# Gate and up products of the last two token blocks as seven Strassen products, with block 1's feed-forward shared out over two mixes

## The chip, the cores and the metric

The kernel runs on one core of one Trainium2 chip. The metric is the device time of one execution in microseconds (us), lower is better. Of the kernel before there are three timed runs and one profiled execution.

## The reference, cut to what matters

The reference is one layer of a hybrid decoder. A prompt of 2048 tokens and a sample group of 64 tokens go through the same weights, all in float32. Per layer, on h of 1024 columns:

```python
z, xbc, dt_raw, q, k, v = split(rmsnorm(h, g_mix) @ w_in)
mix = concat(ssd_branch(z, xbc, dt_raw, ...), swa_banded(q, k, v, sinks, rel_bias))
h = h + mix @ w_out
h = h + cross_attention(rmsnorm(h, g_cross), mem_k, mem_v, w_cq, w_co)
hn = rmsnorm(h, g_ffn)
h = h + (silu(hn @ w_gate) * (hn @ w_up)) @ w_down      # 1024 -> 2816 -> 1024
y = rmsnorm(h, g_final)
```

The last-but-one line, the feed-forward, is what the change is about. Both kernels must give y of both groups and the new states and caches.

## The kernel before, in words

**Numbers as pairs.** A float32 operand is held as a high part (rounded to the fp32r format) and the rest, so each 128x128 piece of a product takes three TensorE matmuls of 512 columns: high x high, rest x high, high x rest (`multiply`, L2642 to L2644). Tokens are the 512 moving columns. Activations stand with the feature on the partition.

**Blocks.** The prompt is cut into four blocks of 512 tokens (0 to 3). A block has the stages I (input projection), mix (SSD scan and window attention), W (w_out), Q (cross query), cross attention, O (w_co), F (feed-forward: gate and up for each of 22 slices f of 128 hidden features, and `down` in groups of four slices, FG).

**Panels.** All weights come in panels of up to 1024 columns: SyncE loads a panel into `w_raw` (ring of three), ScalarE rounds it into `w_hi` (`round_panel`, L1641), VectorE takes the rest into `w_lo` (`low_panel`, L2037). Both do this two panels ahead of TensorE (AHEAD), at the head of each step of the order that `panel_order` writes out.

**Hosted work.** The mix of block b+1 is cut into 37 beats: `chain(ssd(b + 1), attention(b + 1))`, 19 beats for the scan and 18 for the attention. Each engine runs one beat after each step of block b's feed-forward, which has 66 steps (44 gate or up, 22 down), most of them 24 matmuls. So blocks 0, 1 and 2 host the mixes of blocks 1, 2 and 3.

**An attention unit** u (of 8) has an A beat and a B beat. In A, TensorE transposes the probabilities of unit u-1 (L2768) and forms the scores of unit u (L2783). VectorE adds the bias (L2276), takes maxima (L2284 to L2290), and ScalarE takes four exponentials (L1781). In B, VectorE normalises (L2299, semaphore `pn`, for which the transposes of the next A wait) and TensorE multiplies unit u-1 with the values (L2795). All queues run in program order:

```python
for p, step in enumerate(STEPS):           # ScalarE
    round_panel(n + AHEAD)
    if late is not None: round_hidden(late) # hid_h of the slice finished a step before
    ...                                     # silu of a gate step
    if p >= 1: next(mix, None)              # one beat
```

**Last block.** Block 3's feed-forward has nothing to host. `last_ffn` runs it alone, with panels of four outputs and two k, and works the sample group's 64 tokens through the same panels (`sample`, L2934 and L2935; `turn_sample`). Before it stands the third norm: squares and their sums (L1653, L2066), token sums (L2659), the reciprocal root and the diagonal (L2080), its row (L2664, L2085), then `norm3_t`, `norm3_hi`, `norm3_lo` (L2374, L1852, L2379).

**Engines besides.** GpSimd has almost nothing to do after the start: two copies and subtractions (L701, L705, L1627, L1629). Block b's y is turned and stored in the W stage of block b+1 (`turn_y`), block 3's at the end.

## Time and profile before

| what | us |
| --- | --- |
| timed runs: median (lowest to highest of 3) | 2883.46 (2878.35 to 2885.44) |
| span of the profiled execution | 2881.1 |
| what lies around it, if that execution took the median | 2.4 |
| TensorE matmul busy | 2775.2 (96%) |
| VectorE busy | 1561.8 (54%) |
| ScalarE busy | 1170.1 (41%) |
| GpSimd busy | 33.8 (1%) |
| HBM read and written | 277.90 MB and 23.85 MB, 105 GB/s |

The profile is one execution. The busy time of an engine is the union of its instructions. A matmul's time in a row runs from its start to its modelled end, so it is longer than the distance to the next one, which is what counts for throughput. PEclk is the granted clock of TensorE, 1.00 for 2.4 GHz and 0.50 for 1.2 GHz. A time in square brackets is what the engine was idle before the instruction, with the instruction that released it.

### The profile page before, as it was taken

The numbers are of one execution on the slowest core, as the hardware profiler recorded it, in microseconds if no ns is written. First come the engines' busy times: TensorE is split into PE (matmuls) and PEld (weight loads), VectorE is DVE, ScalarE is ACT, GpSimd is POOL, SyncE is SP. The second block draws the span as 40 slices with busy tenths as digits, with TensorE's granted clock in tenths as the row PEclk, the third lists the DMA queues.
The fourth block names the chain that finished last, engine by engine and source line by source line (L and its number), as shares of the span: only waits on it lengthen the run. The fifth ranks groups of instructions, "written<-read, shape, count | busy, mean of one in ns | idle before, by whom it ended". The sixth has DMA issues, their size and how long they took to land. (4 is left out here: it accounts for less than half of the span.)

```text
span 2881.1 us, 34707 instructions
## 1 busy us (share of the span) xinstructions
PE 2775.2 (96%) x13539; PEld 2248.0 (78%) x13539; DVE 1561.8 (54%) x2591; ACT 1170.1 (41%) x1878; POOL 33.8 (1%) x53
## 2 busy tenths in 40 slices
PE   6799789999999999999999999999999987999998
PEld 4478667888878888888778888888778876888886
DVE  4455665667653386667553576666643555333334
ACT  3455644543452255443542246444532333222222
POOL 2100000000000000000000000000000000000000
PEclk9899989999999999999999999999999998999998
DMA  9643554222223354222223353222223331222221
GB/s 306 228 127 117 168 144 124 81 82 76 81 72 92 100 176 110 81 84 74 74 88 95 103 172 99 82 73 80 75 88 99 119 122 52 80 81 81 81 81 60
DMA packets 415094, 303.05 MB, mean 105 GB/s; under 512 B 48075, under 2 KB 384079, under 8 KB 413890
## 3 DMA queue, kind: packets, MB, share of 16 engines
q1 hardware_dynamic: 412474, 294.41, 33.9%
q10 hardware_dynamic: 1880, 6.34, 0.6%
q8 instruction: 108, 1.77, 0.3%
q14 instruction: 56, 0.46, 0.1%
q0 software_dynamic: 576, 0.07, 0.0%
HBM read 277.90 MB, written 23.85 MB: 105 GB/s over the span
## 5 line engine op out<-in xcount | busy, mean ns | idle before, releaser
L2037 DVE TENSOR_TENSOR w_lo<-w_raw,w_hi 128x1024 fp32r<-128x1024 f32 x398 | 486.6, 1224 | 526.4 <-ACT w_hi L1641 524.7
L1641 ACT ACTIVATE w_hi<-w_raw 128x1024 fp32r<-128x1024 f32 x398 | 419.2, 1054 | 538.0 <-PE L L2644 260.5
L2642 PE MATMUL L<-xa_h,w_hi 128*128 128x512 f32 x1184 | 474.3, 401 | 0.0
L2643 PE MATMUL L<-xa_h,w_lo 128*128 128x512 f32 x1184 | 463.6, 392 | 0.0
L2644 PE MATMUL L<-xa_l,w_hi 128*128 128x512 f32 x1184 | 463.3, 391 | 0.0
L2642 PEld LDWEIGHTS L<-xa_h,w_hi 128*128 128x128 f32 x1184 | 223.6, 189 | 54.0 <-issue 6.7
L2644 PEld LDWEIGHTS L<-xa_l,w_hi 128*128 128x128 f32 x1184 | 223.5, 189 | 48.0
L2643 PEld LDWEIGHTS L<-xa_h,w_lo 128*128 128x128 f32 x1184 | 223.7, 189 | 45.9 <-issue 1.0
L2642 PE MATMUL L<-xb_h,w_hi 128*128 128x512 f32 x576 | 230.8, 401 | 9.6 <-DVE xb_l L2056 9.6
L2644 PE MATMUL L<-xb_l,w_hi 128*128 128x512 f32 x576 | 225.6, 392 | 0.0
L2643 PE MATMUL L<-xb_h,w_lo 128*128 128x512 f32 x576 | 225.5, 392 | 0.0
L2642 PE MATMUL L<-hid_h,w_hi 128*128 128x512 f32 x528 | 210.9, 399 | 1.2 <-DVE hT L2596 1.2
L2643 PE MATMUL L<-hid_h,w_lo 128*128 128x512 f32 x528 | 206.1, 390 | 0.0
L2644 PE MATMUL L<-hid_l,w_hi 128*128 128x512 f32 x528 | 205.9, 390 | 0.0
L2596 DVE TENSOR_TENSOR hT<-L,hT 128x512 f32<-128x512 f32 x144 | 99.4, 690 | 137.0 <-PE L L2644 136.5
L2954 PE MATMUL G<-xa_h,w_hi 128*128 128x512 f32 x352 | 139.0, 395 | 3.1 <-DVE xa_l L2379 3.1
L2955 PE MATMUL G<-xa_h,w_lo 128*128 128x512 f32 x352 | 138.4, 393 | 0.0
L2956 PE MATMUL G<-xa_l,w_hi 128*128 128x512 f32 x352 | 138.2, 392 | 0.0
L2642 PEld LDWEIGHTS L<-xb_h,w_hi 128*128 128x128 f32 x576 | 108.8, 189 | 35.0 <-POOL flip L1624 6.7
L2644 PEld LDWEIGHTS L<-xb_l,w_hi 128*128 128x128 f32 x576 | 108.8, 189 | 23.3
L2643 PEld LDWEIGHTS L<-xb_h,w_lo 128*128 128x128 f32 x576 | 109.0, 189 | 21.3 <-issue 0.7
L2642 PEld LDWEIGHTS L<-hid_h,w_hi 128*128 128x128 f32 x528 | 99.1, 188 | 28.1 <-issue 3.5
(570 smaller groups left out, 4518.5 us busy)
## 6 DMA issues: line engine op xcount, KB each, us to landing
w_raw<-in_w_down_dram SPq DMA_DIRECT2D x88, 512.0 KB, 3.4
w_raw<-in_w_gate_dram SPq DMA_DIRECT2D x66, 512.0 KB, 3.8
w_raw<-in_w_up_dram SPq DMA_DIRECT2D x66, 512.0 KB, 3.8
w_raw<-in_w_in_dram SPq DMA_DIRECT2D x56, 512.0 KB, 3.8
xt<-xT_dram SPq DMA_DIRECT2D x56, 256.0 KB, 3.9
w_raw<-in_w_gate_dram SPq DMA_DIRECT2D x44, 256.0 KB, 2.8
w_raw<-in_w_up_dram SPq DMA_DIRECT2D x44, 256.0 KB, 3.1
fwin<-in_w_in_dram SPq DMA_DIRECT2D x8, 1156.0 KB, 10.2
```

The costliest lines, as they stand in the source:

```text
L1641: act.activation(w_hi[:, n % RING, 0:w], w_raw[:, n % RING, 0:w], ACT.Copy)\
L2037: dve.tensor_tensor(w_lo[:, n % RING, 0:w], w_raw[:, n % RING, 0:w], w_hi[:, n % RING, 0:w].bitcast(F32), ALU.subtract).then_inc(s["lo_rea ...
L2596: dve.tensor_tensor(hT[:, n, :], bank(bank_of[o]), hT[:, n, :], ALU.add)\
L2642: pe.matmul(acc, wh, rh, start=(k == 0), stop=False)
L2643: pe.matmul(acc, wl, rh, start=False, stop=False)
L2644: last = pe.matmul(acc, wh, rl, start=False, stop=(k == kn - 1))
L2954: pe.matmul(bank(m), wh, rh, start=(first and k == 0), stop=False)
L2955: pe.matmul(bank(m), wl, rh, start=False, stop=False)
L2956: last = pe.matmul(bank(m), wh, rl, start=False, stop=(final and k == 2 * qs - 1))
```

## The change

**Order of blocks.** Block 0's feed-forward hosts block 1's mix as before. Block 1's feed-forward is cut in two: slices 0 to 10 host the mix of block 2, slices 11 to 21 that of block 3 (FORDER[1] and FORDER[2], 34 steps each, groups of 4, 4 and 3 slices, so that four of the down steps have 18 matmuls). The 37 beats fit in 33 steps because four steps (TWO_BEATS) take two beats. Block 1's normed input and h go to DRAM and come back (`xah_dram`, `xal_dram`, `h_dram`); block 2's normed input goes to DRAM as `xn_dram`.

**Gate and up of blocks 2 and 3 together.** After block 3's O stage, 22 units (a unit is 256 columns of w_gate or of w_up) are each taken as a 2x2 block product: the weights' quadrants are a half of the input features by 128 outputs, the activations' quadrants a half of the features by one of the two token blocks. Seven products of quadrant sums (p1 to p7, 12 matmuls each) replace eight. Of the weights, GpSimd forms four sums per unit (`sums`). Of the activations, four sums per k (`mixed`) are formed once, from block 2's normed input out of DRAM and block 3's from `third`. The results are put together by VectorE (`put_c11`, `put_c12`, `put_c21`, `put_c22`), the hidden values go to DRAM (`store_hidden`).

**Down of blocks 2 and 3** follows, each with its own pass over w_down (stage D), one block's 22 slices accumulated in PSUM. The hidden values come back from DRAM and are split again. The sample group's gate and up are worked out once per unit with 256 columns in place of 512 (`sample_unit`). Block 2's y is turned within block 3's down.

What each part is: `load_unit` loads 1 MB of raw weights, ScalarE's `unit_hi` and VectorE's `unit_lo` split them (`ghi`, `glo`), `sum_hi` and `sum_lo` split the four sums.

```diff
+FG = {0: [(0, 4), (4, 8), (8, 12), (12, 16), (16, 20), (20, 22)],
+      1: [(0, 4), (4, 8), (8, 11), (11, 15), (15, 19), (19, 22)]}
+FORDER = {0: ([("gu", f) for f in range(0, 5)] + [("d", 0)] + [("gu", f) for f in range(5, 9)] + [("d", 1)]
+              + [("gu", f) for f in range(9, 13)] + [("d", 2)] + [("gu", f) for f in range(13, 17)] + [("d", 3)]
+              + [("gu", f) for f in range(17, 22)] + [("d", 4), ("d", 5)]),
+          1: ([("gu", f) for f in range(0, 5)] + [("d", 0)] + [("gu", f) for f in range(5, 9)] + [("d", 1)]
+              + [("gu", 9), ("gu", 10), ("d", 2)]),
+          2: ([("gu", f) for f in range(11, 16)] + [("d", 3)] + [("gu", f) for f in range(16, 20)] + [("d", 4)]
+              + [("gu", 20), ("gu", 21), ("d", 5)])}
+FFN_OF = {0: 0, 1: 1, 2: 1}
...
-            order += [("E", b, step) for step in last_steps()]
+            order += [("F", FFN_OF[b], step) for step in ffn_steps(b)]
+    for b in (2, 3):
+        order += [("D", b, (half, q)) for half in range(2) for q in range(DQ)]
     return order
 
...
+            TWO_BEATS = (21, 24, 27, 30)
+            def mix_beats(b, p):
+                return 0 if p == 0 else 2 if b >= 1 and p in TWO_BEATS else 1
...
+                def load_unit(u):
+                    if u >= 2:
+                        sp.wait_ge(s["u_S"], FROM["u_S"] + 4 * (u - 1))
+                        sp.wait_ge(s["u_lo"], FROM["u_lo"] + 2 * (u - 1))
+                    w = w_up if u % 2 else w_gate
+                    c0 = (u // 2) * 256
+                    sp.dma_start(uraw[u % 2][:], w[:, c0:c0 + 256].rearrange("(k p) n -> p k n", p=P))\
+                      .then_inc(s[f"u_in{u % 2}"], 16)
...
+                    if A0 + 14 <= n < A0 + 14 + KT:
+                        k = n - A0 - 14
+                        sp.wait_ge(s["n3_l"], 2 * KT)
+                        sp.dma_start(xah_dram.ap()[:, k * TB:k * TB + TB], xa_h[:, k, :].bitcast(F32))\
+                          .then_inc(s["xa_out"], 16)
+                        sp.dma_start(xal_dram.ap()[:, k * TB:k * TB + TB], xa_l[:, k, :].bitcast(F32))\
+                          .then_inc(s["xa_out"], 16)
...
+                    if 0 <= n - pos[("I", 3, ("v", 0))] < 4:
+                        m = n - pos[("I", 3, ("v", 0))]
+                        if m == 0:
+                            sp.wait_ge(s["xa_out"], 32 * KT)
+                            sp.wait_ge(s["o_lo"], 3 * C)
+                        for part, there in ((xa_h, xah_dram), (xa_l, xal_dram)):
+                            sp.dma_start(part[:, 2 * m:2 * m + 2, :].bitcast(F32),
+                                         there.ap()[:, 2 * m * TB:2 * (m + 1) * TB].rearrange("p (k t) -> p k t", t=TB))\
+                              .then_inc(s["xa_in"], 16)
...
+                def sums(u):
+                    raw = uraw[u % 2]
+                    a11, a12, a21, a22 = raw[:, 0:4, 0:P], raw[:, 4:8, 0:P], raw[:, 0:4, P:256], raw[:, 4:8, P:256]
+                    s1, s2, s3, s4 = (Sr[:, i, :].rearrange("p (k n) -> p k n", n=P) for i in range(4))
+                    pool.wait_ge(s[f"u_in{u % 2}"], FROM[f"u_in{u % 2}"] + 16 * (u // 2 + 1))
+                    if u >= 1:
+                        pool.wait_ge(s["c_lo"], FROM["c_lo"] + 4 * u)
+                    pool.tensor_tensor(s1, a21, a22, ALU.add).then_inc(s["u_S"], 1)
+                    pool.tensor_tensor(s3, a11, a21, ALU.subtract).then_inc(s["u_S"], 1)
+                    pool.wait_ge(s["u_S"], FROM["u_S"] + 4 * u + 1)
+                    pool.tensor_tensor(s2, s1, a11, ALU.subtract).then_inc(s["u_S"], 1)
+                    pool.wait_ge(s["u_S"], FROM["u_S"] + 4 * u + 3)
+                    pool.tensor_tensor(s4, a12, s2, ALU.subtract).then_inc(s["u_S"], 1)
+                def mixed(i):
+                    o = stg[i % 2]
+                    b11, b21 = x2p[:, 2 * (i % 2), :], x2p[:, 2 * (i % 2) + 1, :]
+                    for e in range(2):
+                        pool.wait_ge(s[f"x2_in{2 * (i % 2) + e}"], 16 * (i // 2 + 3))
+                    if i >= 2:
+                        pool.wait_ge(s["t_lo"], FROM["t_lo"] + 5 * (i - 1))
+                    pool.wait_ge(s["x3_t"], FROM["x3_t"] + 2 * i + 1)
+                    pool.tensor_tensor(o["T1"][:], o["B12"][:], b11, ALU.subtract).then_inc(s["bt"], 1)
+                    pool.wait_ge(s["x3_t"], FROM["x3_t"] + 2 * i + 2)
+                    pool.tensor_tensor(o["T3"][:], o["B22"][:], o["B12"][:], ALU.subtract).then_inc(s["bt"], 1)
+                    pool.wait_ge(s["bt"], FROM["bt"] + 4 * i + 1)
+                    pool.tensor_tensor(o["T2"][:], o["B22"][:], o["T1"][:], ALU.subtract).then_inc(s["bt"], 1)
+                    pool.wait_ge(s["bt"], FROM["bt"] + 4 * i + 3)
+                    pool.tensor_tensor(o["T4"][:], b21, o["T2"][:], ALU.subtract).then_inc(s["bt"], 1)
...
+                    if b == 2:
+                        act.dma_start(xn_dram.ap()[:, i, :], T2[:, i % 2, :]).then_inc(s[f"xn_out{i % 2}"], 16)
+                        return
...
+                def mixed_hi(i):
+                    for n, name in enumerate(("B22", "T1", "T3", "T2", "T4")):
+                        if n == 0:
+                            act.wait_ge(s["x3_t"], FROM["x3_t"] + 2 * i + 2)
+                        else:
+                            act.wait_ge(s["bt"], FROM["bt"] + 4 * i + n)
+                        act.activation(xc_h[name][:, i, :], stg[i % 2][name][:], ACT.Copy).then_inc(s["t_hi"], 1)
...
+                def third(i):
+                    o = stg[i % 2]
+                    if i >= 2:
+                        dve.wait_ge(s["bt"], FROM["bt"] + 4 * (i - 1))
+                        dve.wait_ge(s["t_lo"], FROM["t_lo"] + 5 * (i - 1))
+                    for e, name in enumerate(("B12", "B22")):
+                        k = i + 4 * e
+                        dve.scalar_tensor_tensor(o[name][:], hT[:, k, :], g_of(PV_FFN, k), RB, ALU.mult, ALU.mult)\
+                           .then_inc(s["x3_t"], 1)
+                def mixed_lo(i):
+                    for n, name in enumerate(("B22", "T1", "T3", "T2", "T4")):
+                        dve.wait_ge(s["t_hi"], FROM["t_hi"] + 5 * i + n + 1)
+                        dve.tensor_tensor(xc_l[name][:, i, :], stg[i % 2][name][:], xc_h[name][:, i, :].bitcast(F32),
+                                          ALU.subtract).then_inc(s["t_lo"], 1)
...
+                def put_c22(u):
+                    j = u // 2
+                    dve.wait_ge(s["p5"], FROM["p5"] + u + 1)
+                    dve.wait_ge(s["u3_ev"], FROM["u3_ev"] + u + 1)
+                    dve.wait_ge(s["c21_ev"], FROM["c21_ev"] + u + 1)
+                    if u % 2 == 0:
+                        dve.wait_ge(s["h_out2"], FROM["h_out2"] + 16 * j)
+                        dve.tensor_tensor(gq[:, 2, :], u3[:], bank(5), ALU.add).then_inc(s["c22_ev"], 1)
+                    else:
+                        dve.tensor_tensor(u3[:], u3[:], bank(5), ALU.add).then_inc(s["c22_ev"], 1)
+                        dve.wait_ge(s["g_ev"], FROM["g_ev"] + 4 * j + 3)
+                        dve.drain()
+                        dve.tensor_tensor(gq[:, 2, :], gq[:, 2, :], u3[:], ALU.mult).then_inc(s["h_ev"], 1)
...
+                def product(acc, w, x, ks, begin, end, more_on=False):
+                    for k in ks:
+                        wh, wl = w(k)
+                        xh, xl = xc_h[x][:, k, :], xc_l[x][:, k, :]
+                        pe.matmul(acc, wh, xh, start=(begin and k == 0), stop=False, skip_group_check=more_on)
+                        pe.matmul(acc, wl, xh, start=False, stop=False, skip_group_check=more_on)
+                        last = pe.matmul(acc, wh, xl, start=False, stop=(end and k == 3), skip_group_check=more_on)
+                    return last
...
+                def p1(u):
+                    pe.wait_ge(s["u_lo"], FROM["u_lo"] + 2 * u + 1)
+                    if u % 2 == 0 and u >= 2:
+                        pe.wait_ge(s["g_ev"], FROM["g_ev"] + 4 * (u // 2 - 1) + 1)
+                    elif u >= 3:
+                        pe.wait_ge(s["h_ev"], FROM["h_ev"] + 4 * ((u - 3) // 2) + 1)
+                    product(bank(u % 2), own(0, 0), "B11", ALL, True, True).then_inc(s["p1"], 1)
+                def p2(u):
+                    pe.wait_ge(s["u_lo"], FROM["u_lo"] + 2 * u + 2)
+                    pe.wait_ge(s["t1_ev"], FROM["t1_ev"] + u + 1)
+                    product(bank(u % 2), own(1, 0), "B21", ALL, False, True, True).then_inc(s["p2"], 1)
+                def p3(u):
+                    pe.wait_ge(s["c_lo"], FROM["c_lo"] + 4 * u + 4)
+                    pe.wait_ge(s["c22_ev"], FROM["c22_ev"] + u + 1)
+                    product(bank(5), mixed(3), "B22", ALL, False, True, True).then_inc(s["p3"], 1)
...
+                def p6(u, ks=ALL):
+                    pe.wait_ge(s["c_lo"], FROM["c_lo"] + 4 * u + 1)
+                    if u >= 1:
+                        pe.wait_ge(s["u2_ev"], FROM["u2_ev"] + u)
+                    return product(bank(3), mixed(0), "T2", ks, True, True)
...
+                def gate_up():
+                    for i in range(4):
+                        pe.wait_ge(s["t_lo"], FROM["t_lo"] + 5 * (i + 1))
+                        for fn, sem in ((p4, "p4"), (p6, "p6"), (p7, "p7"), (p5, "p5")):
+                            last = fn(0, range(i, i + 1))
+                            if i == 3:
+                                last.then_inc(s[sem], 1)
+                    for u in range(1, UNITS):
+                        p1(u)
+                        p3(u - 1)
+                        p4(u).then_inc(s["p4"], 1)
+                        p2(u)
+                        sample_unit(u)
+                        p6(u).then_inc(s["p6"], 1)
+                        p7(u).then_inc(s["p7"], 1)
+                        if u % 2 == 1:
+                            turn_sample(u // 2)
+                        p5(u).then_inc(s["p5"], 1)
+                    p3(UNITS - 1)
```

The instruction order shows what moved. `L2596` and `L3101`, `L2037` and `L2392`, `L2299` and `L2658`, `L2276` and `L2635` are the same lines before and after.

VectorE in the feed-forward of block 1, from the bias addition of attention unit 2 to that of unit 3 (first the kernel before):

```order
L2276 TENSOR_TENSOR SC<-G,bias 128x1024
L2284 TENSOR_REDUCE sm<-SC 128x4
L2287 TENSOR_TENSOR sm<-sm,snk 128x4
L2289 TENSOR_SCALAR sm<-sm 128x4
L2290 TENSOR_TENSOR sm<-snk,sm 128x4
L2596 TENSOR_TENSOR hT<-L,hT 128x512 x2
L2037 TENSOR_TENSOR w_lo<-w_raw,w_hi 128x1024
L2295 TENSOR_TENSOR sm<-sm 128x4
L2297 RECIPROCAL sm<-sm 128x4
L2299 TENSOR_TENSOR SC<-SC,sm 128x1024
L2306 TENSOR_TENSOR q_l<-G,q_h 128x2x128
L2037 TENSOR_TENSOR w_lo<-w_raw,w_hi 128x1024
```

```order
L2643 TENSOR_REDUCE sm<-SC 128x4
L2646 TENSOR_TENSOR sm<-sm,snk 128x4
L2648 TENSOR_SCALAR sm<-sm 128x4
L2649 TENSOR_TENSOR sm<-snk,sm 128x4
L3101 TENSOR_TENSOR hT<-L,hT 128x512 x2
L2392 TENSOR_TENSOR w_lo<-w_raw,w_hi 128x1024
L2654 TENSOR_TENSOR sm<-sm 128x4
L2656 RECIPROCAL sm<-sm 128x4
L2658 TENSOR_TENSOR SC<-SC,sm 128x1024
L2665 TENSOR_TENSOR q_l<-G,q_h 128x2x128
L2635 TENSOR_TENSOR SC<-G,bias 128x1024
```

Before, a whole step (its `w_lo` is the last row) stood between unit 2's normalisation and unit 3; now unit 3 follows at once.

ScalarE at the end of slice 10, the last before group d2 (`down` of slices 8 to 10), in the changed kernel. `SC,sm` are the exponentials of attention unit 6, the second `hid_h` is slice 10:

```order
L2027 ACTIVATE PT<-G 128x1024
L2031 ACT_TABLE_LOAD
L2031 ACTIVATE SC,sm<-SC,sm 128x256 x4
L2033 ACTIVATE sm<-sm 128x4
L1891 ACTIVATE w_hi<-w_raw 128x768
L2351 ACTIVATE hid_h<-sg 128x512
L2039 ACTIVATE q_h<-G 128x2x128
```

Before, the down groups inside block 1's feed-forward used slices that were at least a step older:

```order
L1777 ACTIVATE PT<-G 128x1024
L1781 ACTIVATE SC,sm<-SC,sm 128x256 x4
L1783 ACTIVATE sm<-sm 128x4
L1641 ACTIVATE w_hi<-w_raw 128x1024
L1789 ACTIVATE q_h<-G 128x2x128
```

The rounding of slice 10 now stands behind the exponentials and a panel, and the down step that reads it stands next on TensorE.

VectorE after block 3's third norm. Before, the pairs of `norm3_t` and `norm3_lo`, and now `third` and `mixed_lo` (`st_` and `x2p` are raw sums and block 2's input, `xh_`, `xl_` their parts):

```order
L2379 TENSOR_TENSOR xa_l<-T_96,xa_h 128x512
L2374 SCALAR_TENSOR_TENSOR T_96<-hT,pv,diag 128x512
L2379 TENSOR_TENSOR xa_l<-T_96,xa_h 128x512
L2374 SCALAR_TENSOR_TENSOR T_96<-hT,pv,diag 128x512
L2379 TENSOR_TENSOR xa_l<-T_96,xa_h 128x512 x2
```

```order
L2790 SCALAR_TENSOR_TENSOR st_B_168<-hT,pv,diag 128x512
L2790 SCALAR_TENSOR_TENSOR st_B_169<-hT,pv,diag 128x512
L2796 TENSOR_TENSOR xl_B_135<-st_B_163,xh_B_128 128x512
L2796 TENSOR_TENSOR xl_T_136<-st_T_164,xh_T_129 128x512
L2796 TENSOR_TENSOR xl_T_138<-st_T_165,xh_T_131 128x512
L2796 TENSOR_TENSOR xl_T_137<-st_T_166,xh_T_130 128x512
L2796 TENSOR_TENSOR xl_T_139<-st_T_167,xh_T_132 128x512
```

For each of four k there are now two products and five remainders on VectorE, with the four sums on GpSimd between them.

## Rows read from the trace of the kernel before

**Rows 1.** The page: busy time, share of the span and instructions.
```profile
PE 2775.2 (96%) x13539; PEld 2248.0 (78%) x13539; DVE 1561.8 (54%) x2591; ACT 1170.1 (41%) x1878; POOL 33.8 (1%) x53
```
**Rows 2.** Windows: us, busy of PE, PEld, DVE, ACT, POOL, PEclk, DMA share, GB/s.
```profile
2000.00:2100.00 100.00, 100.00 (x530) 78.24 (x529) 61.14 (x96) 56.89 (x112) 0.00 (x0) 1.00 0.24 72
...
2428.40:2850.00 421.60, 421.60 (x1899) 341.28 (x1898) 145.04 (x183) 107.75 (x146) 0.00 (x0) 1.00 0.24 77
```
**Rows 3.** Timeline of PE, start and us, 24 matmuls of 512 columns apart (W stage).
```profile
2303.56 0.39 PE L2642 MATMUL L<-ym_h,w_hi 128*128 128x512 f32 x1
...
2309.00 0.39 PE L2642 MATMUL L<-ym_h,w_hi 128*128 128x512 f32 x1
```
**Rows 4.** Timeline of DVE: attention units 0, 1 and 4 of block 3's mix.
```profile
2006.29 1.23 DVE L2276 TENSOR_TENSOR SC<-G,bias 128x1024 f32<-128x1024 f32 x1 [2.74 <-PE G L2783]
...
2014.73 1.23 DVE L2299 TENSOR_TENSOR SC<-SC,sm 128x1024 f32<-128x1024 f32 x1
...
2019.23 1.23 DVE L2276 TENSOR_TENSOR SC<-G,bias 128x1024 f32<-128x1024 f32 x1
...
2027.15 1.23 DVE L2299 TENSOR_TENSOR SC<-SC,sm 128x1024 f32<-128x1024 f32 x1
...
2061.79 1.23 DVE L2276 TENSOR_TENSOR SC<-G,bias 128x1024 f32<-128x1024 f32 x1 [2.10 <-PE G L2783]
...
2070.22 1.23 DVE L2299 TENSOR_TENSOR SC<-SC,sm 128x1024 f32<-128x1024 f32 x1
```
**Rows 5.** Timeline of PE in block 2's feed-forward: the same units 0 and 1.
```profile
2006.17 0.50 PE L2642 MATMUL L<-xa_h,w_hi 128*128 128x512 f32 x1
...
2011.79 0.39 PE L2642 MATMUL L<-hid_h,w_hi 128*128 128x512 f32 x1
...
2017.26 1.03 PE L2768 MATMUL G<-ident,SC 128*128 128x128 f32 x8
...
2024.83 1.08 PE L2795 MATMUL G<-PT,vtok 128*64 128x256 f32 x8
```
**Rows 6.** Timeline of ACT, unit 4: rounding of a panel and of a hidden slice.
```profile
2066.93 1.04 ACT L1641 ACTIVATE w_hi<-w_raw 128x1024 fp32r<-128x1024 f32 x1
...
2069.86 0.63 ACT L1997 ACTIVATE hid_h<-sg 128x512 fp32r<-128x512 f32 x1
```
**Rows 7.** Windows around the idle times of PE in block 3, columns as in rows 2.
```profile
2325.00:2329.00 4.00, 0.48 (x4) 0.06 (x2) 2.64 (x4) 2.19 (x3) 0.00 (x0) 1.00 0.41 131
2329.50:2336.30 6.80, 6.80 (x19) 5.54 (x20) 2.84 (x16) 0.00 (x0) 0.00 (x0) 0.50 0.00 0
...
2414.80:2428.40 13.60, 7.05 (x14) 4.24 (x15) 10.12 (x25) 3.29 (x6) 0.00 (x0) 0.50 0.00 1
```
**Rows 8.** Timeline of PE from block 3's last O matmul to its feed-forward.
```profile
2410.46 0.39 PE L2644 MATMUL L<-cq_l,w_hi 128*128 128x512 f32 x1
...
2423.42 0.76 PE L2954 MATMUL G<-xa_h,w_hi 128*128 128x512 f32 x1 [3.10 <-DVE xa_l L2379]
```
**Rows 9.** Timeline of DVE at the end of the third norm, blocks 3 and 2.
```profile
2420.36 0.69 DVE L2085 COPY diag<-G 128x512 f32<-128x512 f32 x1 [2.17 <-PE G L2664]
...
1862.27 1.23 DVE L2037 TENSOR_TENSOR w_lo<-w_raw,w_hi 128x1024 fp32r<-128x1024 f32 x1 [0.26 <-ACT w_hi L1641]
```
**Rows 10.** DMA issues: KB each, median us to landing.
```profile
xt<-xT_dram SPq DMA_DIRECT2D x56, 256.0 KB, 3.9
...
mem<-in_mem_prompt_dram SPq DMA_DIRECT2D x1, 1024.0 KB, 5.5
```
**Rows 11.** Groups of POOL, mean ns and idle before; then DVE's timeline beside L1629.
```profile
L701 POOL TENSOR_TENSOR stT<-stT,edS 128x512 f32<-128x512 f32 x8 | 8.0, 1039 | 22.9 <-DVE xS L999 22.9
...
L1629 POOL TENSOR_TENSOR kml<-kmT,kmh 128x1024 fp32r<-128x1024 f32 x1 | 3.2, 3233 | 0.1
...
232.20 1.73 DVE L2037 TENSOR_TENSOR w_lo<-w_raw,w_hi 128x1024 fp32r<-128x1024 f32 x1
```

1047 lines of the change are left out of this document (720 added, 327 removed).

## The prediction

> **What bounds the kernel now.** I read the page's busy times first. TensorE is busy 96% of the span; VectorE 54%, ScalarE 41%, GpSimd 1% [rows 1]. So the kernel runs at TensorE's pace, unless a stage says otherwise. The windows say the same by stage: while block 2's feed-forward hosts attention TensorE is busy 100 of 100 us at clock 1.00, with VectorE at 61 and ScalarE at 57; in block 3's lone feed-forward it is busy 421.6 of 421.6 us with VectorE at 145 [rows 2]. There a matmul less is time less. Twenty-four matmuls of 512 columns lie (2309.00 - 2303.56) / 24 = **0.2267 us** apart [rows 3]; that is the price of one. What TensorE loses, it loses between the stages, by gaps and by the clock after them; and the hosted stages stay full only because the chain of the attention is covered. These two the change touches.
>
> **The change part by part.**
>
> *Products.* Gate and up of blocks 2 and 3 were 2 x 44 steps of 24 = 2112 matmuls; now 22 units x 7 x 12 = 1848. 264 x 0.2267 = **-59.9 us**. The sample's 176 matmuls fewer of 512 columns are replaced by 352 of half the width: nothing. Nothing else on TensorE is dropped: block 1's gate, up and down, and down of blocks 2 and 3, are the same matmuls in another order. Does TensorE stay the bound within the units? A unit is 84 x 0.2267 + 16 x 0.113 = 20.9 us. VectorE has two remainders of 1024 columns, four of 512 and six or seven sums of 512 out of PSUM, at 1.23 and 0.69 about 10.5 us; GpSimd four sums of 512, 4.2 us at 1.04 (that price is argued below); ScalarE less than VectorE. Yes, by a factor of two.
>
> *Attention with less cover: +42.* Before, two steps lie between one unit's scores and the next unit's transposes; at TWO_BEATS only one does. The chain from the bias addition to the end of the normalisation is 2006.29 to 2014.73 + 1.23 = 9.67 us for unit 0, 9.15 for unit 1, 9.66 for unit 4, in which hidden slices are rounded too [rows 4]. TensorE's cover is one step, 2006.17 to 2011.79 = 5.6, and the product with the values, 1.08 (none beside unit 0) [rows 5]. So TensorE waits 9.67 - 5.6 = 4.1 at p = 21, 9.15 - 6.7 = 2.45 at p = 24 and 9.66 - 6.7 = 3.0 at p = 27. Queued behind the waiting transposes is the next unit's score and with it its chain, so the loss isn't caught up. At p = 30 two things meet. Group d2 stands right behind slice 10, whose `hid_h` waits on ScalarE for unit 6's exponentials and a panel: in the row of unit 4 ScalarE is free of both 2066.93 + 1.04 - 2061.79 = 6.2 us after the addition [rows 6]; with `hid_h` 0.63 and the remainder 0.69 it is 7.5. TensorE comes to slice 10 after six matmuls, 1.5 us: 6.0 lost. VectorE's additions of that delayed step then stand ahead of unit 6's normalisation: an estimated 2.5 more. The last remainder of the attention, for which W waits, adds 1.7. Together 4.1 + 2.45 + 3.0 + 6.0 + 2.5 + 1.7 = 20 per host; the second host's d5 also has the squares for the norm, 1.0 each: 22. Bounds: 30, if the chain loses a third where TensorE waits; 50, if VectorE's panel remainder is always caught behind the additions.
>
> *The clock after a gap: +13.6.* In the W stage of block 3 TensorE did 0.48 of 4.00 us at clock 1.00; the stretch behind it, 6.8 us, ran at 0.50, that is 1.2 GHz [rows 7]. It costs half of itself, 3.4. I count the two gaps of each host that are over 3.5 us (4.1 and 6.0), 4 x 3.4. Bounds 0 (hosted gaps lie too far apart to matter) and 24 (seven gaps do).
>
> *From the third norm to gate and up: +16.4.* Before: 2423.42 - 2410.46 = 12.96 us idle [rows 8] and 13.6 us at 0.50 about it, of which I put 2.5 to work done at the low clock: 15.4 [rows 7]. Now VectorE has the norm's row at 2420.36 + 0.69, 10.6 after the last O matmul [rows 9]. Behind it stand three `sum_lo` (3 x 0.69) and the first `third` (0.75), with 0.6 for the hand-overs: T1 starts at 14.0. Then 16 GpSimd operations in a row, 16 P. Unit 1 can't be loaded before, since block 2's input lies where its weights go: 1 MB, 5.5 us to landing [rows 10], rounding 1.04, remainder 1.23. TensorE has 72 matmuls of unit 0 and its sample part to do meanwhile, 18.1 us. Lost: 14.0 + 16 P + 7.8 - 18.1 + 2.5 = 6.2 + 16 P. P is 1.04 in GpSimd's one group of 512 columns; beside a remainder on VectorE, 1024 columns took 3.23, half of that is 1.6, and VectorE's own remainder stretched from 1.23 to 1.73 [rows 11]. Here VectorE is working all the time, so P = 1.6: 31.8 - 15.4 = **+16.4**. By P = 1.04 it would be +7.4. The upper bound is mutual exclusion: in each k, VectorE's 5 x 0.69 + 2 x 0.75 = 4.95 on top of 4 x 1.04 makes 2.27 per sum: +27. The Trainium skill speaks against the change here, in "GPSIMD Engine Reference", section "8. Key points": GpSimd and VectorE share their interface to SBUF and contend when VectorE reads two SBUF inputs. By that rule mutual exclusion, the upper bound, would hold, and GpSimd would be a poor home for sums on the critical path; rows 11 agree that both stretch, though by less than full exclusion.
>
> *The rest: +3.* Block 1's normed input goes out and comes back in 256 KB pieces (3.9 us to landing [rows 10]) while hundreds of steps lie between: 0. Block 2's third norm must wait for its stores before a buffer of `T2` is used again; its last panel remainder ends at 1863.5 [rows 9], 4.5 before TensorE's next need: 0 to 5, I take 1.5. The turn from gate and up to down: the last `put_c22` and the store and return of the hidden values; down begins with slices that are long there: 1.5 at the end for filling PSUM banks. DMA traffic rises by some tens of MB, on queues at 0.24 of their time [rows 2]: nothing.
>
> Sum: -59.9 + 42 + 13.6 + 16.4 + 3 = **+15.1**. Against the profiled execution 2881.1 + 15.1 = 2896.2 of span; that execution stands 2.4 under the median of the runs, which I add: **2898.5 us**. A measurement of this kernel tells about 0.3% (8.7 us) from no change: faster is below 2875, slower above 2892.
>
> **The rivals.**
>
> *A, the attention hides itself: 2854.* The place is the one step at p = 21, 24, 27 and 30. The chain of 9.66 holds a panel's rounding and remainder and a hidden slice (1.04 + 1.23 + 0.63 = 2.9). If these do not stand on it, it is 6.8, just the 6.7 that TensorE has to do; that is the point from which it decides. Then per host 1.2 + 0.1 + 0.1 + 3.1 + 2.5 + 1.7, some 9 to 10, so 20 in all, and no gap is long enough for the clock. With the prologue at P = 1.04: -59.9 + 20 + 7.4 + 3 = -29.5. For it: matmuls saved are certain, and all else is slack. Against it: in the order of both engines panel and hidden slice do stand between exponentials and normalisation.
>
> *B, a wash: 2876 to 2890.* Waits as forecast, but the clock stays up (0) and P = 1.04: -59.9 + 42 + 7.4 + 3 = -7.5 (2876); with one of the two as forecast, up to 2889.6. For it: the gaps of the hosts are 20 us apart with full work between; the fall in [rows 7] is at a change of stage.
>
> *C, GpSimd and VectorE exclude each other: 2928.* P = 2.27 in the prologue (+27), the units' sums stretch but stay hidden, and each of seven gaps per host drops the clock (24) with waits at the upper bound (50): -59.9 + 50 + 24 + 27 + 3 = +44.
>
> That the change doesn't do what it says is out: the order has 264 matmuls of these fewer and the two-beat steps as described.
>
> **How the numbers follow.** Forecast 0.46 (2885 to 2912 on its own), A 0.22, B 0.22, C 0.10. Of the forecast's 0.46 I give 0.40 to slower and 0.06, its lower end, to no change; of B's 0.22 0.20 to no change and 0.02 to faster; A is faster, C slower. Faster 0.22 + 0.02 = 0.24, same 0.06 + 0.20 = 0.26, slower 0.40 + 0.10 = 0.50. The range goes from 2858, which leaves out half of A, to 2928, which leaves out half of C.
>
> **What would show it.** TensorE's instructions: gate and up of blocks 2 and 3 at 20.9 us per unit, full. In each host four gaps before L3274 of about 4, 2.5, 3 and 2.5 us, ended by VectorE's L2658, and one of 6 inside d2 and d5 ended by the `hid_l` of slices 10 and 21, two of the five with the clock at 0.50 behind them. From block 3's O to the first products: T1 14 us after the last O matmul, 16 sums on GpSimd at 1.6 each. The forecast is wrong if L3274 doesn't wait after a two-beat step, if the sums take 1.04 beside VectorE, or if TensorE waits within the units (then GpSimd or VectorE is the bound there, which none of the cases holds).

## The result, and the profile after

| what | before | after |
| --- | --- | --- |
| median of the runs (lowest to highest) | 2882.06 us (2878.35 to 2885.44, 4 runs) | 2911.56 us (2910.02 to 2913.88, 4 runs) |
| span of the profiled execution | 2881.1 us | 2912.2 us |
| TensorE matmul busy | 2775.2 us | 2736.2 us |
| ratio after / before, 95% interval | | 1.0108 [1.0093, 1.0123] |

The changed kernel is 29.5 us slower. The forecast was 2898.5, within a range of 2858 to 2928, so the sign was right and the size half; the result lies at the very top of what the forecast had as its own case (2885 to 2912). The page, with the lines that answer to [rows 1]:

```profile
PE 2736.2 (94%) x13451; PEld 2224.2 (76%) x13451; DVE 1609.2 (55%) x2679; ACT 1179.0 (40%) x1948; POOL 172.6 (6%) x157
...
PE   6799789999999999999889999889769999989998
...
PEclk9899999999999999999999999999889999999999
```

TensorE is busy for 39 us less, and the span is 31 us longer. (Its work fell by more, 61 us by the table below; matmuls at the low clock last longer.) The row of PE shows where to look: the two pairs of 8 are the ends of the two hosted halves of block 1's feed-forward, the 7 and 6 are block 3's cross attention and the start of gate and up, the 8 that follows them is the turn to down. The windows of these stretches, columns as in [rows 2]:

```profile
1380.00:1500.00 120.00, 100.66 (x502) 76.76 (x501) 63.99 (x104) 48.85 (x111) 0.00 (x0) 0.90 0.20 59
1850.00:1972.00 122.00, 100.16 (x509) 76.42 (x509) 71.33 (x120) 53.91 (x120) 0.00 (x0) 0.93 0.15 46
2170.00:2600.00 430.00, 430.00 (x2088) 362.83 (x2087) 196.56 (x280) 130.58 (x210) 100.81 (x80) 1.00 0.22 74
```

The units themselves are full: 430 of 430 us at clock 1.00, VectorE at 46%, GpSimd at 23% with 100.81 / 80 = 1.26 us per sum. The hosted ends, full before, now lack some 20 us each and run at 0.90 and 0.93.

**Where the time went.** A matmul's usual distance to the next is that of most of its kind (0.227 us at 512 columns). What a stretch takes beyond the sum of these is lost. I split it into distances over 0.95 us (gaps), the excess of those under the clock of 0.50, and the small rest:

| stretch | forecast | measured | how it comes out of the two traces |
| --- | --- | --- | --- |
| matmuls | -59.9 | -60.8 | sum of the usual distances, 2643.0 before, 2582.2 after |
| gaps in the two hosts | +42 | +42.3 | 20.0 (1380 to 1500) + 22.3 (1850 to 1972), none before |
| low clock in the two hosts | +13.6 | +22.8 | 13.2 + 9.6, none before |
| third norm to gate and up | +16.4 | +22.7 | 34.2 (2104.6 to 2170) less 11.5 (2410.5 to 2430 before); the first wait behind O, 2.3 in both, is left out of both |
| turn to down | +3, with all the rest | +10.3 | 2600 to 2630 |
| rest | | -6.2 | mostly small distances in the attention, 12.9 + 12.9 before, 8.9 + 10.4 after |
| sum | +15.1 | +31.1 | 2912.2 - 2881.1 |

The lines between these terms are not sharp. With the usual distance taken by line, tiles and shape of the matmul, as their median, the same traces give -62.1 for the matmuls, and for the two hosts 44.3 of gaps and 19.5 of low clock: 63.8 in all, beside the 65.1 of the table.

**The gaps in the host.** Timeline of TensorE, the matmul after each of the five largest gaps in the first host, with what ended the wait:

```profile
1386.72 0.69 PE L3274 MATMUL G<-ident,SC 128*128 128x128 f32 x2 [4.05 <-DVE SC L2658]
...
1415.20 0.55 PE L3274 MATMUL G<-ident,SC 128*128 128x128 f32 x3 [2.52 <-DVE SC L2658]
...
1442.60 0.55 PE L3274 MATMUL G<-ident,SC 128*128 128x128 f32 x3 [3.07 <-DVE SC L2658]
...
1467.56 0.80 PE L3148 MATMUL L<-hid_h,w_hi 128*128 128x512 f32 x1 [5.71 <-DVE hid_l L3074]
...
1476.32 0.55 PE L3274 MATMUL G<-ident,SC 128*128 128x128 f32 x3 [1.90 <-DVE SC L2658]
```

The waits were forecast at 4.1, 2.45, 3.0, 6.0 and 2.5. The fourth ends with the remainder of slice 10, the others with VectorE's normalisation, as named. The sixth, forecast at 1.7 before W, is a distance of 1.66 at 1496.7. ScalarE and VectorE at that fourth wait:

```profile
1464.84 0.49 ACT L2031 ACTIVATE SC<-SC,sm 128x256 f32<-128x256 f32 x1
1465.24 0.19 ACT L2031 ACTIVATION_READ_ACCUMULATOR SC<-SC,sm 128x1 f32 x1
1465.34 0.19 ACT L2033 ACTIVATE sm<-sm 128x4 f32<-128x4 f32 x1
1465.43 0.83 ACT L1891 ACTIVATE w_hi<-w_raw 128x768 fp32r<-128x768 f32 x1
1466.16 0.61 ACT L2351 ACTIVATE hid_h<-sg 128x512 fp32r<-128x512 f32 x1
```

```profile
1460.30 1.23 DVE L2635 TENSOR_TENSOR SC<-G,bias 128x1024 f32<-128x1024 f32 x1 [1.03 <-PE G L3289]
...
1466.81 0.69 DVE L3074 TENSOR_TENSOR hid_l<-sg,hid_h 128x512 fp32r<-128x512 f32 x1 [3.49 <-ACT hid_h L2351]
```

The hidden slice is rounded behind the exponentials and a panel, and its remainder ends 1466.81 + 0.69 - 1460.30 = 7.2 us after the bias addition; 7.5 was forecast.

**From the third norm to the units.** GpSimd's first sum, the two it had to wait for and the last, then VectorE: the products of the first two k and the remainders of the first:

```profile
2117.62 1.64 POOL L1867 TENSOR_TENSOR st_T<-st_B,x2p 128x512 f32<-128x512 f32 x1 [14.10 <-DVE st_B L2790]
...
2131.67 1.64 POOL L1867 TENSOR_TENSOR st_T<-st_B,x2p 128x512 f32<-128x512 f32 x1 [0.72 <-DVE st_B L2790]
...
2140.51 1.63 POOL L1867 TENSOR_TENSOR st_T<-st_B,x2p 128x512 f32<-128x512 f32 x1 [2.17 <-DVE st_B L2790]
...
2145.59 1.59 POOL L1873 TENSOR_TENSOR st_T<-x2p,st_T 128x512 f32<-128x512 f32 x1
```

```profile
2116.70 4.78 DVE L2790 SCALAR_TENSOR_TENSOR st_B<-hT,pv,diag 128x512 f32<-128x512 f32 x4
2121.40 1.75 DVE L2796 TENSOR_TENSOR xl_B<-st_B,xh_B 128x512 fp32r<-128x512 f32 x1
2123.07 6.75 DVE L2796 TENSOR_TENSOR xl_T<-st_T,xh_T 128x512 fp32r<-128x512 f32 x4
```

The first sum starts 2117.62 - 2104.51 = 13.1 us after the last O matmul (14.0 forecast); a sum takes 1.67 (1.6 forecast). But VectorE pays more: in the first k its remainders take 6.75 / 4 = 1.69 us in place of some 0.6, and GpSimd then waits for it twice (0.72 and 2.17). In the second and third k, where GpSimd stands still for a part of the time, four of them take 5.70 and 5.72 us, and in the last, with GpSimd silent, 2.48. So the sixteen sums last 29.6 us, 1.85 each.

A second part of this stretch came out longer than forecast. From the end of the last sum (2145.59 + 1.59 = 2147.18) to the first matmul of unit 1 (2159.15) it is 12.0 us, where the forecast has 7.8. SyncE, ScalarE, VectorE and TensorE on this way:

```profile
2147.21 0.38 SPq L1615 DMA_DIRECT2D uraw<-in_w_up_dram  x1
...
2152.03 1.28 ACT L2154 ACT_TABLE_LOAD   x1
...
2154.30 2.01 ACT L2129 ACTIVATE ghi<-uraw 128x1024 fp32r<-128x1024 f32 x2 [0.38 <-issue]
...
2156.56 0.69 DVE L2848 TENSOR_TENSOR gq<-u,G 128x512 f32<-128x512 f32 x1
2157.17 3.06 DVE L2775 TENSOR_TENSOR glo<-uraw,ghi 128x1024 fp32r<-128x1024 f32 x2
...
2159.15 0.50 PE L3402 MATMUL G<-xh_B,ghi 128*128 128x512 f32 x1 [2.89 <-DVE glo L2775]
```

The weights are there for GpSimd at 2152.88, 5.7 after the issue, as forecast. But ScalarE comes to their rounding only at 2154.30, behind the function table and the gate of unit 0, and VectorE to the remainder at 2157.17, behind three results of unit 0.

**The turn to down.** TensorE's product p3 of the last unit needs `put_c22` (L2808). In VectorE's queue it stands behind the remainders of hidden slices 4 to 7, whose data SyncE had only just asked for:

```profile
2610.80 2.20 SPq L1628 DMA_DIRECT2D hraw<-hid_dram  x4
...
2613.51 0.63 ACT L2177 ACTIVATE xh_T<-hraw 128x512 fp32r<-128x512 f32 x1 [6.65 <-DMA hraw<-hid_dram]
2614.70 0.68 DVE L2870 TENSOR_TENSOR xl_T<-hraw,xh_T 128x512 fp32r<-128x512 f32 x1
...
2618.16 0.68 DVE L2808 TENSOR_TENSOR u<-u,G 128x512 f32<-128x512 f32 x1
...
2618.99 0.76 PE L3402 MATMUL G<-xh_B,sh_h 128*128 128x512 f32 x1 [7.58 <-DVE u L2808]
```

### The profile page after: what moved, and what is told of

It reads as the page before. It is cut to its first block and busy times, and to the rows that moved or that the text cites. A ratio compares the mean times of both kernels' runs of the same rounds, so it can differ in the third digit from the quotient of the medians.

```text
span 2912.2 us, 35273 instructions
## 1 busy us (share of the span) xinstructions
PE 2736.2 (94%) x13451; PEld 2224.2 (76%) x13451; DVE 1609.2 (55%) x2679; ACT 1179.0 (40%) x1948; POOL 172.6 (6%) x157
## 5 line engine op out<-in xcount | busy, mean ns | idle before, releaser
L2392 DVE TENSOR_TENSOR w_lo<-w_raw,w_hi 128x1024 fp32r<-128x1024 f32 (+1 forms) x312 | 379.4, 1217 | 373.8 <-ACT w_hi L1891 372.1
L1891 ACT ACTIVATE w_hi<-w_raw 128x1024 fp32r<-128x1024 f32 (+1 forms) x312 | 326.7, 1048 | 313.5 <-PE L L3150 124.3
L3148 PE MATMUL L<-xa_h,w_hi 128*128 128x512 f32 x832 | 334.8, 402 | 0.0
L3150 PE MATMUL L<-xa_l,w_hi 128*128 128x512 f32 x832 | 325.2, 391 | 0.0
L3149 PE MATMUL L<-xa_h,w_lo 128*128 128x512 f32 x832 | 325.0, 391 | 0.0
L3148 PEld LDWEIGHTS L<-xa_h,w_hi 128*128 128x128 f32 x832 | 156.6, 188 | 37.2 <-issue 4.7
L3150 PEld LDWEIGHTS L<-xa_l,w_hi 128*128 128x128 f32 x832 | 156.6, 188 | 34.0
L3149 PEld LDWEIGHTS L<-xa_h,w_lo 128*128 128x128 f32 x832 | 156.9, 189 | 32.0 <-issue 1.0
L3148 PEld LDWEIGHTS L<-xb_h,w_hi 128*128 128x128 f32 x576 | 109.2, 190 | 34.2 <-POOL flip L1838 6.7
L3101 DVE TENSOR_TENSOR hT<-L,hT 128x512 f32<-128x512 f32 x96 | 65.9, 689 | 85.3 <-PE L L3150 85.1
L3402 PE MATMUL G<-xh_T,sh_h 128*128 128x512 f32 x264 | 105.9, 401 | 0.0
L3404 PE MATMUL G<-xl_T,sh_h 128*128 128x512 f32 x264 | 104.8, 397 | 0.0
```

The lines of the kernel that those rows point to most:

```text
L1891: act.activation(w_hi[:, n % RING, 0:w], w_raw[:, n % RING, 0:w], ACT.Copy)\
L2392: dve.tensor_tensor(w_lo[:, n % RING, 0:w], w_raw[:, n % RING, 0:w], w_hi[:, n % RING, 0:w].bitcast(F32), ALU.subtract).then_inc(s["lo_rea ...
L3101: dve.tensor_tensor(hT[:, n, :], bank(bank_of[o]), hT[:, n, :], ALU.add)\
L3148: pe.matmul(acc, wh, rh, start=(k == 0), stop=False)
L3149: pe.matmul(acc, wl, rh, start=False, stop=False)
L3150: last = pe.matmul(acc, wh, rl, start=False, stop=(k == kn - 1))
```

## The experiments

All are the changed kernel with one edit or a sum of edits. Each is timed against runs of the kernel before on the same chip.

**1. The two-beat steps moved to the scan.**

```diff
-            TWO_BEATS = (21, 24, 27, 30)
+            TWO_BEATS = (6, 8, 10, 12)
...
-                        if p == GATED_ROOT:
+                        root = GATED_ROOT if b == 0 else GATED_ROOT - 4
+                        if p == root:
```

> The four steps with two beats are moved from the attention to the scan (p = 6, 8, 10, 12; the second and third beat of each chunk together). Theory (the attention's chain of 9.7 us has one step of cover instead of two): the gaps before L3274 of 2.9 to 4.5 us go, and with them most of the low clock of the two hosts; what stays is about 2 us at d2 and d5 and 2 before W, per host, and at most 1 to 2 us per scan chunk where the scan's own chain now has one step. Hosts lose some 15 us in gaps and clock in place of 65, so about 2862 us. Rival (the gaps come from more work per step on VectorE and ScalarE in the two hosts, wherever it stands): the gaps only move into the scan, and the time stays within 10 us of 2911.

Measured: 2877.64 us, 0.999 [0.998, 0.9999] of before, 34 us less than the changed kernel. No gap before L3274 is left; 2.3 us remain at d2 and d5 (6.1 before) and 1.7 and 2.3 before W. The rival falls: in the same stretches (1380 to 1500, 1840 to 1952) gaps cost 3.4 + 4.0 us and the low clock 1.5 + 1.5, so both go together. It missed 2862 by 15; a new gap of 5.1 us in each host, with the low clock behind it, makes up for these (2 x 4.9 us over the usual distance and 5.0 of low clock). VectorE there (idle times of TensorE at 1336.86 to 1341.97):

```profile
1333.93 0.69 DVE L2600 TENSOR_TENSOR zs<-yac,G 128x512 f32<-128x512 f32 x1
1335.79 0.17 DVE L2606 TENSOR_SCALAR ssg<-ssg 128x8 f32<-128x8 f32 x1 [1.17 <-ACT sqsum L2007]
...
1339.04 2.19 DVE L2612 TENSOR_SCALAR zs<-zs,ssg 128x256 f32<-128x256 f32 x8
1341.14 1.28 DVE L3102 TENSOR_TENSOR hT<-L,hT 128x512 f32<-128x512 f32 x2
```

The root of the gate is drawn ahead of the step's own work, and the step is now a down step, whose additions (L3102) free TensorE's banks.

**2. The same with the root at a gate step.**

```diff
-            TWO_BEATS = (6, 8, 10, 12)
+            TWO_BEATS = (6, 8, 10, 15)
...
-                        root = GATED_ROOT if b == 0 else GATED_ROOT - 4
+                        root = GATED_ROOT if b == 0 else GATED_ROOT - 3
```

> As e1, but the pairs are at p = 6, 8, 10 and 15 (the two turns of the scan's result together) and VectorE's root of the gate is drawn ahead at step 14, a gate step, in place of step 13, a down step. In e1 a gap of 5.1 us stood before step 14 in both hosts: VectorE worked on the root and eight scalings (5.4 us) ahead of the additions of step 13, for whose banks TensorE waited. Theory: that gap and its low clock go, 2 x (5.1 + 3) less 2, so 2877.6 - 13 = about 2864. Rival (the scan's pairs at p = 10 and 12 made it): a gap of like size at the same place or before the turns, about 2877.

Measured: 2866.94 us, 0.9956 [0.994, 0.9971]. The gap is gone and nothing took its place. So the hosting of two mixes by one feed-forward costs little when the pairs stand where the chains are short: in the hosted stretches 8.9 us of gaps and clock are left of 65, and by the medians the choice of the four steps was worth 2911.56 - 2866.94 = 44.6 us. That is less than the 56 us of gaps and clock that went; some 5 of these came back as small distances in the same stretches. The one wait left inside the first host, TensorE's timeline:

```profile
1452.46 0.50 PE L3149 MATMUL L<-hid_h,w_hi 128*128 128x512 f32 x1 [1.93 <-DVE hid_l L3074]
```

**3. The hidden slice ahead of the exponentials**, the pairs as in the changed kernel.

```diff
                         elif kind == "up":
                             late = f
+                            if b >= 1 and p == 29:
+                                round_hidden(late)
+                                late = None
```

> In the changed kernel, ScalarE rounds the hidden slice 10 (and 21) ahead of unit 6's exponentials and the next panel. Theory (the 6.1 us gaps inside d2 and d5 are that slice waiting on ScalarE behind the exponentials): they fall to 2 to 4 us, with some of the wait moving to unit 6's normalisation, 3 to 7 us less in all. Rival (VectorE's product and remainder, behind the bias addition and maxima, set it): the gaps stay at 5 to 6 us.

Measured, a single run: 2900.59 us beside 2911.56. The wait at d2, forecast at 2 to 4:

```profile
1464.19 0.50 PE L3151 MATMUL L<-hid_h,w_hi 128*128 128x512 f32 x1 [2.14 <-DVE hid_l L3077]
```

The distances fell from 6.1 to 2.5 in both hosts, 7.2 us, and unit 6's wait stayed (2.6 and 3.0). The theory holds, but the 11 us are more than the 3 to 7 it gave. The traces have the low clock for the rest: each gap of 6.1 us in the changed kernel has 6.8 us at 0.50 with it, and neither gap of 2.5 us here has any. How much of the 11 us a second run would repeat isn't known.

**4. The activation sums on VectorE.** GpSimd's `mixed` goes; in `third`:

```diff
+                    b11, b21 = x2p[:, 2 * (i % 2), :], x2p[:, 2 * (i % 2) + 1, :]
+                    for e in range(2):
+                        dve.wait_ge(s[f"x2_in{2 * (i % 2) + e}"], 16 * (i // 2 + 3))
+                    dve.drain()
+                    dve.tensor_tensor(o["T1"][:], o["B12"][:], b11, ALU.subtract).then_inc(s["bt"], 1)
+                    dve.tensor_tensor(o["T3"][:], o["B22"][:], o["B12"][:], ALU.subtract).then_inc(s["bt"], 1)
+                    dve.drain()
+                    dve.tensor_tensor(o["T2"][:], o["B22"][:], o["T1"][:], ALU.subtract).then_inc(s["bt"], 1)
+                    dve.drain()
+                    dve.tensor_tensor(o["T4"][:], b21, o["T2"][:], ALU.subtract).then_inc(s["bt"], 1)
```

> The sixteen activation sums are formed by VectorE instead of GpSimd. Theory (the two engines slow each other: 1.69 us per operation on both sides): VectorE's remainders fall back to 0.69 and its sums take 0.69; per k it has 11 operations, 7.7 us, in place of the 8.7 of now; unit 1 is loaded some 6 us sooner, 5 to 9 us less, about 2904. Rival (VectorE's remainders are slow from something else, such as where their operands lie): they stay at 1.69, VectorE's stretch grows to 4 x 13 us, and the time rises by 10 to 15 us.

Measured: 2906.31 us, 1.0089 [1.0074, 1.0104], 5 us less than the changed kernel. VectorE in the second k:

```profile
2121.82 0.69 DVE L2778 TENSOR_TENSOR st_T<-st_B,x2p 128x512 f32<-128x512 f32 x1
...
2124.59 0.68 DVE L2788 TENSOR_TENSOR xl_B<-st_B,xh_B 128x512 fp32r<-128x512 f32 x1
2125.20 2.49 DVE L2788 TENSOR_TENSOR xl_T<-st_T,xh_T 128x512 fp32r<-128x512 f32 x4
```

With GpSimd silent the same four remainders take 2.49 us, not 6.75. One engine with eleven operations is faster here than two that share them: counted from the last O matmul, the last sum ends 6.9 us sooner and unit 1 begins 6.4 us sooner. The rival falls.

**5. The two engines in turn**, neither beside the other: GpSimd's sums wait for both products of their k, VectorE's remainders for all four sums, and the products of the next k stand behind the remainders.

```diff
-                    pool.wait_ge(s["x3_t"], FROM["x3_t"] + 2 * i + 1)
+                    pool.wait_ge(s["x3_t"], FROM["x3_t"] + 2 * i + 2)
...
                 def mixed_lo(i):
+                    dve.wait_ge(s["bt"], FROM["bt"] + 4 * (i + 1))
...
-                    for i in range(5):
-                        if i < 4:
-                            third(i)
-                        if i >= 1:
-                            mixed_lo(i - 1)
+                    for i in range(4):
+                        third(i)
+                        mixed_lo(i)
```

> In the changed kernel GpSimd's four sums of a k and VectorE's seven operations of it are put one behind the other, never side by side (VectorE's remainders wait for all four sums, and the next k begins when they are done). Theory (the two engines take their turns at one interface: beside each other 4 of each took 6.75 us, alone 4 x 0.62 + 4 x 1.04 = 6.6): each sum falls from 1.67 to about 1.04 us, each remainder from 1.69 to 0.62, and nothing is lost by not overlapping: the 16 sums end within 3 us of the 29.6 us they take now, and the time stays within 5 us of the changed kernel. Rival (they only slow each other in part, overlap still gains): a sum alone takes 1.3 or more, and the stretch grows by over 5 us.

Measured, a single run: 2918.39 us, 6.8 more than the changed kernel; beside the one run of the kernel before on its chip (2885.36) it is 33.0 more, where the changed kernel had 29.5. GpSimd, then VectorE, in the second k:

```profile
2128.54 1.27 POOL L1867 TENSOR_TENSOR st_T<-st_B,x2p 128x512 f32<-128x512 f32 x1 [4.63 <-DVE st_B L2790]
2129.77 1.28 POOL L1869 TENSOR_TENSOR st_T<-st_B,st_B 128x512 f32<-128x512 f32 x1
```

```profile
2134.28 2.49 DVE L2797 TENSOR_TENSOR xl_T<-st_T,xh_T 128x512 fp32r<-128x512 f32 x4
```

A sum alone takes 1.27, not 1.04, and a remainder alone 0.62. So full exclusion would be 4 x (1.27 + 0.62) = 7.6 us for four of each; side by side they took 6.75. The sixteen sums now last 34.2 us (2118.85 to 2153.08), 4.7 more. Overlap of sums and remainders gains about a tenth, no more. The expectation (within 3 us, a sum at 1.04) fell, though the rival's 1.3 and 5 us were not reached either. Whether the whole kernel stays within 5 us a single run can't tell.

**6. The last `put_c22` ahead of the hidden slices.**

```diff
-                    for h in range(4):
-                        hidden_lo(h)
-                    low_panel(DFIRST, NPAN)
-                    low_panel(DFIRST + 1, NPAN)
-                    for h in range(4, 8):
-                        hidden_lo(h)
-                    put_c22(UNITS - 1)
+                    hidden_lo(0)
+                    hidden_lo(1)
+                    put_c22(UNITS - 1)
+                    low_panel(DFIRST, NPAN)
+                    hidden_lo(2)
+                    hidden_lo(3)
+                    low_panel(DFIRST + 1, NPAN)
+                    for h in range(4, 8):
+                        hidden_lo(h)
```

> Only VectorE's order at the turn from gate and up to down is changed: the last put_c22 and the first panel remainder stand before the remainders of hidden slices 2 to 7. Theory (the 7.97 us gap is VectorE standing in hidden_lo of slices 4 to 7, whose transfer had just been issued, ahead of the put_c22 that p3 of the last unit waits for): gap 1 to 3 us, no or a shorter low-clock stretch behind it, 6 to 9 us less, about 2904. Rival (TensorE waits for data of down, not for that queue order): p3 comes earlier but the same time is lost before the first matmul of down, 2911.

Measured: 2909.73 us, 1.0103 [1.0087, 1.0118]; 1.8 us less than the changed kernel, within what such medians scatter. The trace shows both halves of it: the gap of 7.97 is 1.26, and gaps of 2.07, 2.57 and 0.92 us stand in the first down steps. The queue order was the cause of the big gap, and most of the gain was given back.

**7. Both last puts ahead.** On top of 6:

```diff
                     low_panel(DFIRST + 1, NPAN)
+                    put_c12(UNITS - 1)
                     for h in range(4, 8):
                         hidden_lo(h)
...
-                    put_c12(UNITS - 1)
```

> As e2, and put_c12 too stands ahead of the remainders of slices 4 to 11. In e2 the gap of 7.97 fell to 1.26 but 2.07 + 2.57 + 0.92 us came back in the first down steps, where the last put_c12, its store and the loads queued behind that store on SyncE stood behind the remainders. Theory: these go as well, the turn loses 2 to 3 us in all, 8 us less than the changed kernel, about 2903. Rival (the return of the hidden values by DRAM bounds the first down steps, in whatever order): the small gaps stay, about 2909.

Measured: 2907.74 us, 1.01 [1.0086, 1.0114]. Of the small gaps one of 2.06 stayed, and another of 3.40 came at 2645. That is near the rival's 2909 and not the 2903 of the theory, but the hidden values are not what the second gap waits for: it ends with the remainder of a weight panel, and ScalarE had stood 8.79 us until that panel landed. The loads around it are tested in 9.

**8. All three: 2, 4 and 7 together.**

> Pairs and root as in e5, sums of the activations on VectorE as in e3, puts as in e6. The three places lie apart, so the gains should add: 2864 - 5 - 8 = about 2851, 1.0% below the kernel before. If they overlap (the same wait moved on), 2858 to 2864.

Measured: 2854.25 us, **0.9918 [0.9906, 0.9931]**, faster than both kernels. It missed 2851 by 3, and its trace has a gap of 4.50 us in the down steps. In that stretch the DMA view shows a burst (window 2580 to 2602, 5.47 MB):

```profile
w_raw<-in_w_down_dram SPq DMA_DIRECT2D x5, 512.0 KB, 13.3
hT<-h_dram SPq DMA_DIRECT2D x2, 1024.0 KB, 11.5
```

A panel lands 13.3 us after its issue; over the whole changed kernel such a panel took 3.6.

**9. The return of h spread out**, and **10. the third panel ahead of hidden slices 8 to 11**, each on top of the last.

```diff
-                    if p == 6:
+                    if p in (8, 10):
...
-                        for tiles, there in halves(2):
-                            sp.dma_start(tiles, there).then_inc(s["h2_in"], 16)
-                    if p == 7:
+                        tiles, there = halves(2)[(p - 8) // 2]
+                        sp.dma_start(tiles, there).then_inc(s["h2_in"], 16)
+                    if p == 13:
```

In the tenth, in ScalarE's and in VectorE's `down` (where the same panel is then left out of the first step):

```diff
+                    round_panel(DFIRST + 2, NPAN)
                     for h in range(8, 12):
                         hidden_hi(h)
...
+                    low_panel(DFIRST + 2, NPAN)
                     for h in range(8, 12):
                         hidden_lo(h)
```

> e7 with the return of h of block 2 (2 x 1 MB) and the two row loads moved from the first down steps to later ones. In e7 the panel for the step after the 4.5 us gap landed some 13 us after its issue, in a burst of 5.5 MB in 22 us on the same queue. Theory: panels land in about 4 us again, the gap of 4.5 us goes with what low clock follows it, 4 to 6 us less than e7, about 2849. Rival (the panel was issued late, since SyncE waited for VectorE): the gap stays and so does the time.

> e9, and the third panel of down is rounded and its remainder taken ahead of hidden slices 8 to 11. Theory: the gap of 2.16 us before the third down step (VectorE's w_lo behind those slices) goes, some 2 us less than e9. Rival: slices 4 to 11 are then late themselves, no change.

Measured: 2854.60 us, 0.9904 [0.9889, 0.9918], and 2852.72 us, 0.9898 [0.9882, 0.9915]. The gap of 4.5 is gone from the ninth's trace, as expected, but the medians of 8 and 9 are the same; against their own runs of before the ratios differ by 0.14%, which these intervals can't tell. So the 4 to 6 us of the expectation were not found, and that this gap was why 8 missed by 3 is not shown. In the tenth the gap of 2.4 before the third step went and one of 2.5 two steps later took its place: no change that can be told. The hosted ends in the tenth, to be read against the two windows above:

```profile
1380.00:1500.00 120.00, 116.79 (x603) 91.64 (x602) 76.49 (x117) 56.50 (x110) 0.00 (x0) 1.00 0.41 118
1830.00:1950.00 120.00, 116.03 (x614) 91.18 (x613) 76.19 (x132) 60.07 (x114) 0.00 (x0) 1.00 0.34 102
```

**11. One product twice.** Each p1 is computed a second time over the first: 264 matmuls more, the number of eight products.

```diff
+                    product(bank(u % 2), own(0, 0), "B11", ALL, True, True)
                     product(bank(u % 2), own(0, 0), "B11", ALL, True, True).then_inc(s["p1"], 1)
```

> The product p1 of each unit is computed twice (the second overwrites the first), 264 matmuls more, so the number that eight products would have. Theory (the units are bound by TensorE alone): 22 x 12 x 0.2267 = 60 us more, about 2971, less perhaps 2.7 of them that fill the wait before unit 1. Rival (VectorE, GpSimd or the loads set the unit's pace in part): clearly less than 60.

Measured: 2971.26 us, 59.7 more than the changed kernel. So the units are bound by TensorE alone, and the seven products do give back 60 us.

## Why the prediction was right or wrong

- **Products, -59.9:** right (-60.8 in the trace, 59.7 by experiment 11). Within the units VectorE took some 9.6 us of 20.9 (10.5 worked out) and GpSimd 4.9 (4.2, since a sum takes 1.26 there and not 1.04); neither holds TensorE up.
- **Attention with less cover, +42:** right in place, kind and size (42.3). Experiment 1 shows the cover is the cause and experiment 3 that the exponentials hold up slice 10. What the prediction took as given and was not: that two mixes in one feed-forward need these four steps. The cost was the table's, not the split's.
- **Clock, +13.6:** the mechanism right, the term mis-sized. I counted two gaps per host, those over 3.5 us; in the trace 9 of the 11 distances of 2.2 us or more in the two hosts have a stretch at 0.50 with them, 41 us of it in all. It cost 22.8 (half of the 41 would be 20.5), near the upper bound of 24. The row I took as the measure [rows 7] told what one fall costs, not how short a gap can bring one.
- **Third norm to gate and up, +16.4:** measured 22.7; three steps of it failed.
  - "Then 16 GpSimd operations in a row": 25.6 us were forecast, and they last 29.6. The price of one was right (1.67 for 1.6), but they don't come in a row. VectorE's own remainder, read as 1.73 for 1.23 [rows 11], takes 1.69 in place of 0.62 wholly beside GpSimd, so that VectorE becomes what the next k waits for.
  - The load of unit 1, 7.8: measured 12.0. Landing and rounding were priced, and not what ScalarE and VectorE have ahead of it in their queues. No experiment tests this part; in the traces of experiments 4 and 5 it takes 12.5 and 10.4.
  - What the kernel before lost here, 15.4: by the table's count it is 11.5 + 2.3 = 13.8. The prediction took all of 12.96 us between two matmuls [rows 8] for idle, but TensorE works in it. The start (13.1 for 14.0) and the work that TensorE does meanwhile gave some 3.5 us back.
  - That the 1.6 fitted is in part luck. It is half of GpSimd's 3.23 us, which run from 232.94 (the row below), and VectorE's remainder beside it ends at 232.20 + 1.73 = 233.93 [rows 11]. So only 0.99 of the 3.23 us lie beside VectorE.
  - Rival C's exclusion is nearly true of the sums and remainders (6.75 us for what is 7.6 in turn), and its +27 was a fair price for it: experiment 5, which forces the engines apart, loses 3.7 us more in this stretch than the changed kernel, some +26 in all.
- **The rest, +3:** wrong. The turn to down alone cost 10.3. I had priced what down needs and not what VectorE's queue holds ahead of the last `put_c22`: a wait for a transfer. It is the question that the prediction asked of the attention (what is queued behind the waiting instruction) and did not ask here.
- **Rival A** (the attention hides itself) and **B** (clock stays up, sums at 1.04) are out: waits as forecast, clock down, sums at 1.67. B's 1.04 holds for no sum of this change, beside VectorE or alone (1.27).

GpSimd's row in the trace of the kernel before:

```profile
232.94 3.23 POOL L1629 TENSOR_TENSOR kml<-kmT,kmh 128x1024 fp32r<-128x1024 f32 x1
```

Three terms came out 9, 6 and 7 us too low and the small distances 6 too high, together the 16 us by which the sum missed (13.1 by the medians, since the profiled execution of the changed kernel was the longest of its four). The sign comes from the attention and from the way to gate and up, both worked out beforehand; but slower had been given a chance of 0.50 only, and the three larger misses all lay on the side that keeps the sign.
